# A two-layer decoder trunk on one core: x summed in PSUM over the expert sets, 21 weight slots, another load order

## The chip, the cores and the metric

One Trainium2 core runs the whole program. The metric is device time in microseconds (us); the profile is one execution of it. PE is TensorE, DVE VectorE, ACT ScalarE, POOL GpSimd, and SP the engine that issues nearly all the DMAs.

## What is computed

Two layers (DEPTH) over 256 tokens of width 1024, float32. A layer is an attention part and a mixture-of-experts (MoE) part, cut here to the second:

```
x = x + concat[diff attention, stick breaking attention](rms_norm(x)) @ w_out
h2 = rms_norm(x, norm2_g)
# top-1 of 4 expert groups, then top-2 of its 8 experts; 32 experts in all
hg = h2 @ w_gate[e];  hu = h2 @ w_up[e]          # (256, 1024) @ (1024, 256)
x = x + sum_e (silu(hg) * hu * combine[:, e]) @ w_down[e]
```

The weights are read once: 96 MiB of expert matrices in each layer (32 experts, three matrices of 1 MiB), and 16 MiB of w_in and w_out.

## The kernel before

**Slots.** SBUF holds 19 slots of 1 MiB (`wbuf`, SLOT). A slot takes one expert's gate, up or down matrix, or half of one 2 MiB column block of w_in or w_out. An expert set is 4 experts (LANES); 8 sets (SETS) make a layer. A set needs 12 slots. Gate matrices have 8 slots, 4 for each parity of the set; up matrices have 7 (the fourth, slot 9, is shared by both parities); down matrices have 4, shared by both parities. `hT` (the transposed, normed x) and `xn` (the normed x) lie in buffers of their own beside the slots.

**One set.** Each expert of a set gets 32 token places (SLOTS). PE multiplies gathered tokens `hgT` by gate and up (L1366, 128 matmul records), gathers the tokens of the next set by selection matrices (`gather`, L1341), transposes the routing weights (L1350) and the activations (L1387), multiplies by down (L1398) and scatters the result back to token order (L1410, 4 matmuls of 128x512). DVE then adds each of the four scattered blocks to `x_sb` (`into_x`, L916), and PE's next transposes of weights wait for that (`x_moe`). If an expert of a set has more than 32 tokens, `further` runs another round with its own tiles (L1377 is its gate and up). Sets 0 and 1 come in fixed order; sets 2 to 7 are sorted by their fullest expert, fullest first, and in both layers set 2 alone has a second round.

**Routing.** After attention's output projection (L1310), PE computes the router logits (`router`, L1317) and DVE runs a chain of some 30 small instructions from L1057 to L1156. On its way it signals `sel_ready` (PE gathers set 0) and at its end `routed`: only then does PE read the number of tokens and enter the loop over sets, and SP learn which experts sets 2 to 7 are.

**SP's queue.** SP issues DMAs in program order, with waits. `load_first_sets` issues all 12 slots of set 0 and gate and the first three up of set 1 (19 slots) during attention. `load_further_sets` waits for `routed`, reads six numbers and then goes through the sets with waits on `gate_used`, `up_used` and `dn_used`, which ACT counts up when PE has finished with the gate, up and down matrices of a set.

**The first block.** w_in's first 2 MiB block comes in two halves; PE's first projection (L1207) waits for the first, transposes the second half of x, then waits for the rest. Between the first and second projection PE computes `rstd_rows` (L1218) from `rstd_diag` (L994), which DVE makes after it has waited for `gains_in`, six small loads.

## Time and profile before

| | us |
|---|---|
| median of 3 runs | 745.71 (744.35 to 745.98) |
| the profiled execution | 742.31 |
| its span, in which all positions below lie | 740.5 |
| PE busy | 652.9 (88%) |
| DVE busy | 305.3 (41%) |
| ACT busy | 119.0 (16%) |
| HBM read | 237.51 MB, 322 GB/s over the span |

A position such as 170.03 is in microseconds from the start of the span. Layer 0's attention runs to about 153, its routing to 165 and its sets to 374; layer 1's routing is at 515 to 528 and its sets end with the span. PE's busy share is high everywhere, since records of pipelined matmuls touch each other; what limits a stage has to be read from the waits and the DMA rows.

### The profile page before, as it was taken

What the parts mean: (1) busy time and instruction counts of PE and PEld (TensorE: products, weight loads), DVE (VectorE), ACT (ScalarE), POOL (GpSimd) and SP (SyncE); (2) the same over time, 40 slices, a digit from 0 to 9 for tenths busy, and PEclk for the clock granted to TensorE, in tenths of its full rate; (3) what the DMA queues carried; (4) which work ended last, traced back from release to release, by engine and by line L of the source; (5) the groups of instructions that cost most, each with busy time, mean ns of one, the idle gap of its engine ahead of it and who ended that gap; (6) DMA issues with size and microseconds to landing.
All of it is one profiled execution on the core that took longest, in us unless ns stands there. A gap on an engine that the chain in (4) does not pass through costs nothing.

```text
span 740.5 us, 12416 instructions
## 1 busy us (share of the span) xinstructions
PE 652.9 (88%) x4796; PEld 374.1 (51%) x4797; DVE 305.3 (41%) x625; ACT 119.0 (16%) x284; POOL 9.0 (1%) x19
## 2 busy tenths in 40 slices
PE   7999999988798897784999999999898979785966
PEld 4478555475554353432345864546644535443522
DVE  0445663164353443431424377422633434432413
ACT  3103442220000000000031035324000000000000
POOL 0002000000000000000020000000000000000000
PEclk9999999999999998987999999999999999987989
DMA  8798426537999999999999630395299999999995
GB/s 307 264 335 304 169 113 277 234 115 295 415 422 416 393 423 421 421 422 423 388 357 395 271 144 28 129 382 222 67 377 420 422 421 423 422 423 420 423 406 208
DMA packets 52967, 239.09 MB, mean 323 GB/s; under 512 B 7824, under 2 KB 8112, under 8 KB 29376
## 3 DMA queue, kind: packets, MB, share of 16 engines
q1 hardware_dynamic: 52432, 238.14, 80.6%
q0 software_dynamic: 496, 0.44, 0.5%
q8 instruction: 23, 0.38, 0.2%
q14 instruction: 16, 0.13, 0.0%
HBM read 237.51 MB, written 1.05 MB: 322 GB/s over the span
## 4 chain that ended last, share of the span: by engine, by line
PE 67%; DMA 19%; DVE 5%; issue 4%; SPq 2%; DVEq 2%; ACT 1%; ACTq 0%
DMA wbuf<-in_w_down 18%; PE bank L1207 13%; PE bank L1398 11%; PE bank L1366 8%; PE bank L1197 8%; PE bank L1310 7%; PE bank L1410 5%; PE bank L1341 5%; PE bank L1377 2%; DMA wbuf<-in_w_in 1%; SPq L371 1%; PE bank L1266 1%; PE bank L1317 1%; PE bank L1240 1%; PE bank L1286 1%
## 5 line engine op out<-in xcount | busy, mean ns | idle before, releaser
L1398 PE MATMUL bank<-wbuf,qkT 128*32 128x512 f32 x512 | 73.2, 708 | 53.3 <-DMA wbuf<-in_w_down 46.5
L1207 PE MATMUL bank<-wbuf,hTbuf 128*128 128x512 f32 x256 | 114.7, 603 | 3.9 <-DMA wbuf<-in_w_in 3.5
L1366 PE MATMUL bank<-wbuf,qkT 128*32 128x256 f32 x2048 | 113.8, 380 | 2.2 <-DVE qkT L880 2.2
L1366 PEld LDWEIGHTS bank<-wbuf,qkT 128*32 128x32 f32 x2048 | 65.2, 110 | 54.2 <-issue 10.6
L1207 PEld LDWEIGHTS bank<-wbuf,hTbuf 128*128 128x128 f32 x256 | 48.3, 192 | 63.0 <-issue 58.9
L1341 PE MATMUL bank<-qkT,xn 128*128 128x128 f32 x512 | 62.9, 282 | 11.3 <-issue 10.4
L916 DVE TENSOR_TENSOR x_sb<-x_sb,bank 128x512 f32<-128x512 f32 x72 | 49.5, 688 | 51.0 <-PE bank L1410 51.0
L1341 PEld LDWEIGHTS bank<-qkT,xn 128*128 128x128 f32 x512 | 59.9, 196 | 18.4 <-issue 18.4
L1398 PEld LDWEIGHTS bank<-wbuf,qkT 128*32 128x32 f32 x512 | 19.2, 126 | 97.0 <-issue 86.9
L1197 PE MATMUL bank<-hTbuf,wbuf 128*128 128x256 f32 x256 | 56.5, 380 | 0.0
L1310 PE MATMUL bank<-wbuf,hTbuf 128*128 128x512 f32 x128 | 56.1, 594 | 0.0
L1197 PEld LDWEIGHTS bank<-hTbuf,wbuf 128*128 128x128 f32 x256 | 48.2, 190 | 7.0 <-issue 0.7
L908 DVE COPY qkT<-bank 128x512 f32<-128x512 f32 x16 | 11.1, 692 | 77.8 <-PE bank L1398 77.8
L1310 PEld LDWEIGHTS bank<-wbuf,hTbuf 128*128 128x128 f32 x128 | 23.8, 190 | 28.1 <-issue 28.1
L890 DVE RECIPROCAL qkT<-qkT 128x256 f32<-128x256 f32 x18 | 31.6, 1753 | 1.4
L1410 PE MATMUL bank<-qkT 128*128 128x512 f32 x64 | 29.9, 611 | 2.3 <-DVEq L969 2.3
L606 ACT COPY qkT<-bank 128x512 f32<-128x512 f32 x16 | 9.4, 586 | 134.5 <-PE bank L1398 134.5
L1410 PE MATMUL bank<-qkT,hTbuf 128*128 128x512 f32 x64 | 30.3, 616 | 0.0
L904 DVE COPY qkT<-bank 128x256 f32<-128x256 f32 x16 | 6.8, 425 | 53.9 <-PE bank L1387 53.9
L602 ACT ACTIVATE qkT<-bank 128x256 f32<-128x256 f32 x18 | 6.9, 385 | 126.9 <-PE bank L1366 113.1
L1410 PEld LDWEIGHTS bank<-qkT 128*128 128x128 f32 x64 | 11.0, 189 | 21.5 <-issue 17.7
L1410 PEld LDWEIGHTS bank<-qkT,hTbuf 128*128 128x128 f32 x64 | 10.8, 189 | 19.9 <-issue 14.7
(218 smaller groups left out, 564.5 us busy)
## 6 DMA issues: line engine op xcount, KB each, us to landing
wbuf<-in_w_gate SPq DMA_DIRECT2D x64, 1024.0 KB, 14.9
wbuf<-in_w_up SPq DMA_DIRECT2D x64, 1024.0 KB, 17.7
wbuf<-in_w_down SPq DMA_DIRECT2D x56, 1024.0 KB, 14.6
wbuf<-in_w_in SPq DMA_DIRECT2D x24, 1024.0 KB, 14.7
wbuf<-in_w_out SPq DMA_DIRECT2D x8, 1024.0 KB, 6.3
wbuf<-in_w_down SPq DMA_DIRECT2D x16, 512.0 KB, 7.8
x_sb<-in_x SPq DMA_DIRECT2D x2, 512.0 KB, 6.3
out<-x_sb SPq DMA_DIRECT2D x2, 512.0 KB, 2.6
```

What stands on the lines that cost most here:

```text
L606: nc.scalar.copy(dst[:, HALF:], ps[bank][:, :]).then_inc(s["y_a"], 1)
L890: V.reciprocal(rg, rg)
L908: V.tensor_copy(dst[:, 0:HALF], ps[bank][:, :]).then_inc(s["y_d"], 1)
L916: last.append(V.tensor_tensor(x_sb[:, t, c], x_sb[:, t, c], ps[SC_BANK[t][h]][:, :], ALU.add))
L1197: last = MM(ps[PROJ_BANK[i][t]][:, a * SEQ:(a + 1) * SEQ], block_rows(i, k)[:, cols], hT[:, k, :], start=(k == 0), stop=(k == KC - 1))
L1207: last = MM(ps[PROJ_BANK[i][t]][:, :], hT[:, k, t * P:(t + 1) * P], block_rows(i, k), start=(k == 0), stop=(k == KC - 1))
L1310: last = MM(ps[OP_BANK[t][h]][:, :], hT[:, k, t * P:(t + 1) * P], block_rows(i, k), start=(k == 0), stop=(k == KC - 1))
L1341: last = MM(ps[k // 4][:, (k % 4) * P:(k % 4 + 1) * P], xn[:, t, k * P:(k + 1) * P], sel[:, t, :], start=(t == 0), stop=(t == TT - 1))
L1366: last = MM(ps[bank][j * SLOTS:(j + 1) * SLOTS, 0:FF], hgT[:, k, j * SLOTS:(j + 1) * SLOTS], halves[:, at[j], k, :], start=(k == 0), stop= ...
L1377: last = MM(ps[MORE_GU][j * SLOTS:(j + 1) * SLOTS, :].rearrange("p (a f) -> p a f", a=2), hgT_more[:, k, j * SLOTS:(j + 1) * SLOTS], halve ...
L1398: last = MM(ps[banks[h]][j * SLOTS:(j + 1) * SLOTS, :], src[:, c, j * SLOTS:(j + 1) * SLOTS], at[j][:, c * D + h * HALF:c * D + (h + 1) * ...
L1410: MM(ps[SC_BANK[t][h]][:, :], weights[:, t, :], src[:, h * HALF:(h + 1) * HALF], start=True, stop=True).then_inc(s[f"sc{t}{h}_ps"], 1)
```

## The change

- **21 slots.** `xn` and `hT` lose their own buffers and become slots 19 and 20. Slot 19 is then set 1's fourth up matrix, slot 20 the first down matrix of the odd sets. So gate and up are fully double, and the first down matrix too. In attention the same memory serves as `xa` and `hT`, and after it as weights: SP loads up (1,3) after `oT_ps` and down (1,0) after `lg_ps`.
- **x in PSUM.** `keep_x` writes x into four PSUM banks by an identity matmul (4 of 128x512 per layer); every set's scatter accumulates there, and DVE and ACT copy the four banks to `x_sb` once per layer. `into_x` and the `x_moe` waits go. The normed x for the gathers is written over `x_sb` by ACT (`normed_to_x`), after `keep_x`, by way of `xn_first`.
- **Load order.** For set g+1: gate, then all four up, and only then the other three down of set g and the first down of g+1. For the last set down comes before up, and its halves are three instead of four. SP reads one expert number per set, where it read six ahead.
- **Routing.** PE enters the loop after `first_counts`, some ten DVE instructions ahead of `routed`. DVE scales the first half of the gathered set 0 before it sorts the sets, ACT the second half (`first_gathering`). In the loop PE reads the next count after up, not after its activation transposes, and transposes this set's weights there.
- **Router by column halves.** The last token tile of x is transposed and routed in two column halves, with the parameters loaded to match (11 small loads instead of 8).
- **First block in pieces.** The first 1 MiB half of block 0 becomes four DMAs with a semaphore each.
- **PE's loop placed.** In layer 1's second projection 128 semaphore increments stand between the matmuls, which shift all later code of PE.
- A second round shares `hgT`, `y` and the banks of the first, so its scatter ends before the first round's down starts.

```diff
-SLOTS_W = 19
+SLOTS_W = 21
-UP_SLOT = [[4, 5, SLOT_STAGE, 9], [6, 7, 8, 9]]
-DOWN_SLOT = [10, 11, SLOT_VALUES, 16]
+UP_SLOT = [[4, 5, SLOT_STAGE, 9], [6, 7, 8, SLOT_XN]]
+DOWN_SLOT = [[10, 11, SLOT_VALUES, 16], [SLOT_HT, 11, SLOT_VALUES, 16]]
...
             with act.If(most <= SLOTS):
+                act.wait_ge(first["gu_ps"], act.snap(n * LANES))
                 act.sem_inc(gate_used, 1)
             gate(first, n, FIRST_GATE)
...
+            def load_start():
+                for k in range(KC // 2):
+                    sp_.dma_start(dst[:, k, :], src[:, k, :]).then_inc(start_in[k], 16)
...
+            def keep_x(t):
+                for h in range(2):
+                    last = MM(ps[X_BANK[t][h]][:, :], ident, x_sb[:, t, h * HALF:(h + 1) * HALF], start=True, stop=False)
+                last.then_inc(x_kept, 1)
...
+            def scatter(s, n, weights, last):
+                for h in range(2):
+                    pe.wait_ge(s["y_a" if h else "y_d"], n)
+                    for t in range(TT):
+                        mm = MM(ps[X_BANK[t][h]][:, :], weights[:, t, :], y[:, h * HALF:(h + 1) * HALF], start=False, stop=last)
+                        if last:
+                            mm.then_inc(x_ps[t][h], 1)
...
+            def place_loop(n):
+                for _ in range(n):
+                    pe.sem_inc(placed, 1)
...
+                    if l > 0 and i == 1:
+                        place_loop(8)
...
+                # after up, inside the loop
+                pe.wait_ge(routed, l + 1)
+                pe.reg_mov(count, pe.value_load(cnt[0:1, bass.ds(SETS - 1 - g, 1)], min_val=0, max_val=SEQ))
+                transpose_weights(first, n, SELW_BANK)
```

**SP, from the last loads of layer 0's attention to the first ones behind `routed`.** Before:

```order
L368 DMA wbuf<-in_w_up 128x2048
L368 DMA wbuf<-in_w_up 128x2048 [waits oproj_ps]
L368 DMA wbuf<-in_w_up 128x2048
L420 TENSOR_LOAD sorted_i [waits routed]
L420 ISA x2
```

And now:

```order
L364 DMA wbuf<-in_w_up 128x2048 [waits oT_ps]
L360 DMA wbuf<-in_w_gate 128x2048 [waits oproj_ps]
L364 DMA wbuf<-in_w_up 128x2048
L364 DMA wbuf<-in_w_up 128x2048 [waits oproj_ps]
L364 DMA wbuf<-in_w_up 128x2048
L368 DMA wbuf<-in_w_down 128x2048 [waits lg_ps]
L423 TENSOR_LOAD sorted_i [waits routed]
L423 ISA x2
```

One up matrix and one down matrix (1 MiB each) have moved ahead of the wait for `routed`.

**SP, the first turn over the sets, behind the last gate matrix of set 2.** Before:

```order
L364 DMA wbuf<-in_w_gate 128x2048
L368 DMA wbuf<-in_w_up 128x2048 [waits up_used]
L371 DMA wbuf<-in_w_down 128x2048 [waits dn_used]
L371 DMA wbuf<-in_w_down 128x2048 x3
L368 DMA wbuf<-in_w_up 128x2048 x3
L368 DMA wbuf<-in_w_up 128x2048 [waits up_used]
L364 ISA [waits gate_used]
```

And now:

```order
L360 DMA wbuf<-in_w_gate 128x2048
L364 DMA wbuf<-in_w_up 128x2048 [waits up_used]
L364 DMA wbuf<-in_w_up 128x2048 x3
L368 DMA wbuf<-in_w_down 128x2048 [waits dn_used]
L368 DMA wbuf<-in_w_down 128x2048 x3
L423 TENSOR_LOAD sorted_i
L423 ISA x2
L360 ISA [waits gate_used]
```

Eight loads stand between `gate_used` and the wait for `dn_used`, where five stood.

**PE, from the gather of set 0 to its first expert matmul.** The tile qkT holds the selection and the gathered tokens. Before:

```order
L1341 MATMUL bank0<-qkT,xn 128x128 [waits sel_ready,xn_ready]
L1341 MATMUL bank0<-qkT,xn 128x128 x7
L1341 MATMUL bank1<-qkT,xn 128x128 x8
L1350 MATMUL bank6<-cst,qkT 128x128 [waits selw_ready]
L1350 MATMUL bank6<-cst,qkT 128x128
L1549 TENSOR_LOAD sorted_i [waits routed]
L1549 ISA x2
L1550 UNCONDITIONAL_BRANCH
L1550 ISA
L1357 ISA [waits gate_in0]
L1366 MATMUL bank2<-wbuf,qkT 32x256 [waits hg0]
```

And now:

```order
L1379 MATMUL bank0<-qkT,x_sb 128x128 [waits sel_ready,xn_ready]
L1379 MATMUL bank0<-qkT,x_sb 128x128 x7
L1379 MATMUL bank1<-qkT,x_sb 128x128 x8
L1593 TENSOR_LOAD sorted_i [waits first_counts]
L1593 ISA x2
L1594 UNCONDITIONAL_BRANCH
L1594 ISA
L1395 ISA [waits gate_in0]
L1404 MATMUL bank2<-wbuf,qkT 32x256 [waits hg0]
```

The weight transposes have left this place, and the register load waits for an earlier semaphore.

## Rows read from the trace of the kernel before

**Rows 1.** The page: what DMA moved in 40 slices, and the chain by line.

```profile
GB/s 307 264 335 304 169 113 277 234 115 295 415 422 416 393 423 421 421 422 423 388 357 395 271 144 28 129 382 222 67 377 420 422 421 423 422 423 420 423 406 208
...
DMA wbuf<-in_w_down 18%; PE bank L1207 13%; PE bank L1398 11%; PE bank L1366 8%; PE bank L1197 8%; PE bank L1310 7%; PE bank L1410 5%; PE bank L1341 5%; PE bank L1377 2%; DMA wbuf<-in_w_in 1%; SPq L371 1%; PE bank L1266 1%; PE bank L1317 1%; PE bank L1240 1%; PE bank L1286 1%
```

**Rows 2.** Stretches: length, PE, PEld, DVE, ACT, POOL busy, PEclk, DMA share, GB/s.

```profile
160.00:165.00 5.00, 4.03 (x34) 3.82 (x34) 3.97 (x21) 0.37 (x1) 0.00 (x0) 1.00 0.00 0
...
170.00:175.00 5.00, 5.00 (x70) 3.85 (x63) 2.79 (x3) 0.00 (x0) 0.00 (x0) 1.00 0.77 285
...
180.00:185.00 5.00, 5.00 (x33) 1.62 (x26) 1.85 (x4) 0.59 (x1) 0.00 (x0) 1.00 0.99 383
185.00:190.00 5.00, 5.00 (x72) 2.60 (x74) 2.58 (x6) 0.00 (x0) 0.00 (x0) 1.00 0.99 398
...
245.00:250.00 5.00, 3.67 (x8) 1.44 (x8) 2.76 (x4) 0.35 (x1) 0.00 (x0) 1.00 0.86 311
...
545.00:550.00 5.00, 5.00 (x25) 1.58 (x19) 2.44 (x4) 0.59 (x1) 0.00 (x0) 1.00 0.93 346
```

**Rows 3.** Timeline of SP's DMA issues: start, length, instruction, count.

```profile
170.03 2.12 SPq L364 DMA_DIRECT2D wbuf<-in_w_gate  x4
...
182.96 2.68 SPq L371 DMA_DIRECT2D wbuf<-in_w_down  x4
...
231.28 2.08 SPq L364 DMA_DIRECT2D wbuf<-in_w_gate  x4
244.71 2.07 SPq L371 DMA_DIRECT2D wbuf<-in_w_down  x4
...
532.27 3.37 SPq L364 DMA_DIRECT2D wbuf<-in_w_gate  x4
```

**Rows 4.** The chain of waits, layer 0 from routing to set 2.

```profile
164.07 0.03 DVEq L1157
...
165.42 7.11 PE bank L1366 x128
...
193.53 5.18 issue
...
212.16 7.04 PE bank L1366 x128
219.20 0.02 issue
```

**Rows 5.** Timelines, layer 0's routing and second round, then layer 1: idle time before in brackets.

```profile
150.90 0.59 ACT L532 COPY hTbuf<-bank 128x512 f32<-128x512 f32 x1 [0.49 <-PE bank L1170]
...
156.99 0.43 PE L1328 MATMUL bank<-oh,cst 128*128 128x64 f32 x2 [0.77 <-DVEq L1098]
...
160.20 3.81 PE L1341 MATMUL bank<-qkT,xn 128*128 128x128 f32 x32 [0.43 <-DVEq L1122]
...
223.28 7.07 PE L1377 MATMUL bank<-wbuf,hTbuf 128*32 128x512 f32 x64
...
528.09 7.11 PE L1366 MATMUL bank<-wbuf,qkT 128*32 128x256 f32 x128 [0.99 <-DVE qkT L880]
...
582.53 7.07 PE L1377 MATMUL bank<-wbuf,hTbuf 128*32 128x512 f32 x64
```

**Rows 6.** The in-loop register load of PE by its line: min/median/max ns, first and last start.

```profile
L1459 PEldq TENSOR_LOAD <-sorted_i x16: 298/312/318, 177.6 to 727.6; - x16
```

**Rows 7.** The start: timelines of PE and DVE, with the idle time before.

```profile
10.32 5.40 PE L1207 MATMUL bank<-wbuf,hTbuf 128*128 128x512 f32 x8 [3.55 <-DMA wbuf<-in_w_in]
...
16.43 10.46 PE L1207 MATMUL bank<-wbuf,hTbuf 128*128 128x512 f32 x24
...
26.23 0.48 DVE L994 TENSOR_SCALAR wbuf<-cst,rstd 128x128 f32<-128x128 f32 x2 [9.35 <-DMA lamv<-in_lambda_k]
```

**Rows 8.** The chain of waits at the end of the span.

```profile
731.08 1.92 PE bank L1398 x16
733.01 3.73 PE bank L1410 x8
```

More of the change, by code:

```diff
@@ L594, in sb_scales, with weights_copy, first_gathering @@
                 nc.scalar.activation(osq[:, 2 * t + 1, :], osq[:, 2 * t + 1, :], ACT.Exp, scale=-0.5).then_inc(o_rT, 1)
-            def weights_copy(s, n, dst, half):
+            def weights_copy(s, n, dst, bank):
                 act.wait_ge(s["selwT_ps"], n)
-                nc.scalar.copy(dst.rearrange("p t s -> p (t s)"), ps[SELW_BANK][:, half]).then_inc(s["selwT_out"], 1)
+                nc.scalar.copy(dst.rearrange("p t s -> p (t s)"), ps[bank][:, 0:TT * P]).then_inc(s["selwT_out"], 1)
+            def first_gathering(l):
+                act.wait_ge(first["gathered1"], l * SETS + 1)
+                for k in range(4, 8):
+                    last = nc.scalar.activation(hgT[:, k, :], ps[1][:, (k - 4) * P:(k - 3) * P], ACT.Copy,
+                                                scale=g2T[:, k:k + 1])
+                last.then_inc(first["hg1"], 1)
             def gate(s, n, bank):
@@ L1403, in scatter, with down @@
-            def scatter(s, n, weights, src):
-                pe.wait_ge(s["selwT_out"], n)
-                pe.wait_ge(s["y_d"], n)
-                for t in range(TT):
-                    for h in range(2):
-                        if t == 0 and h == 1:
-                            pe.wait_ge(s["y_a"], n)
-                        MM(ps[SC_BANK[t][h]][:, :], weights[:, t, :], src[:, h * HALF:(h + 1) * HALF],
-                           start=True, stop=True).then_inc(s[f"sc{t}{h}_ps"], 1)
+            def down(s, n, parity, src, h, second_half=None):
+                if h == 1 and second_half is not None:
+                    pe.wait_ge(last_dn_in, second_half)
+                at = [slot(DOWN_SLOT[parity][j]) for j in range(LANES)]
+                for c in range(FC):
+                    for j in range(LANES):
+                        last = MM(ps[DN_BANK[h]][j * SLOTS:(j + 1) * SLOTS, :], src[:, c, j * SLOTS:(j + 1) * SLOTS],
+                                  at[j][:, c * D + h * HALF:c * D + (h + 1) * HALF], start=(c == 0), stop=(c == FC - 1))
+                        if c == FC - 1:
+                            last.then_inc(s[f"dn{h}_ps"], 1)
@@ L1542, in _ @@
                 router(l, 1, 1)
-                keep_clock(12)
+                for t in range(TT):
+                    keep_x(t)
                 ranks(l)
```

364 lines of the change are left out of this document (186 added, 178 removed).

## The prediction

> **What bounds the kernel now.** I read the slices of the page first. In the expert sets (slices 11 to 20 and 31 to 39) DMA moves about 421 GB/s, in attention far less [rows 1]. The chain names a down matrix as its largest part: late sets wait for weights. The chain of a layer's first sets is PE's, but DMA is at full rate there too. So I take DMA as the bound of the sets from the moment it restarts after routing, and ask three things: when it restarts, how many slots are then missing, and where it pauses.
>
> A slot of 1 MiB at 421 GB/s takes 2.49 us, a set of 12 slots 29.9. PE needs for a set 7.04 for gate and up, 3.81 for the gather, twice 1.92 for down, 3.73 for the scatter [rows 4, 5, 8] and about 1.2 of small steps: 19.6. It is ahead except at the start of a layer.
>
> - *Restart.* From 160 to 165 DMA moves nothing [rows 2]: all 19 slots are full. SP issues set 2's gate matrices at 170.03 in layer 0 and at 532.27 in layer 1 [rows 3]. That follows the gate matmuls of set 0 (half of the 7.11 us from 165.42 [rows 4], so done at 168.98) and ACT's exponential, 1.05 us later. Until data flows some 2 us pass (170 to 175 lacks 136 of 421 GB/s, 1.6 us).
> - *Missing.* 96 - 19 = 77 slots, 191.7 us.
> - *Pauses.* In layer 0 180 to 190 lacks 38 and 23 GB/s over 5 us each, 0.7 us: down could be issued only at 182.96. 245 to 250 lacks 110, 1.3 us: down at 244.71, after set 2's two rounds. In layer 1 545 to 550 lacks 75, 0.9 us [rows 2, 3].
> - Set 3's gate matrices go out at 231.28, behind set 2's second round (223.28 + 7.07 = 230.35) [rows 3, 5]. DMA has 24 slots to move until there: 170.03 + 2 + 59.8 + 0.7 = 232.5. PE and DMA meet there almost exactly.
>
> **The change part by part.**
>
> *Two more slots: -5.0 us in each layer.* Up (1,3) is issued behind `oT_ps`, down (1,0) behind `lg_ps`; they need 5 us of DMA, which stands empty before the restart. After it 75 slots are missing instead of 77. DMA sets the end, so 2 x 2.49 = 5.0 is all gain.
>
> *Earlier restart: layer 0 -2.0, layer 1 -1.4.* Before, PE entered the loop 1.35 us after `routed` (164.07 to 165.42) [rows 4]. Now its register load waits for `first_counts`, which DVE gives at about 160.8, and PE's sequencer can run it while the gather (160.20 to 164.01 [rows 5]) is in the array: the first in-loop load begins at 177.6 [rows 6], while the gather and transposes before it end at 178.6. The first half of `hgT` is ready near 163.1. ACT's second half starts at 164.0, in four pieces, about 1.2 by the 0.59 us of a copy of 512 columns [rows 5] and twice that at most for short ones; it is needed at 164.05 + 1.8. So gate starts at 164.05, 1.4 earlier; in layer 1 1.1 earlier, since 528.09 lies nearer to its gather's end. ACT signals `gate_used` ahead of its exponential: another 0.3 to 0.6. `routed` itself comes 0.75 later, by the half gather put before the sort, at about 164.9; that is still ahead of gate's end, 167.6.
> Against it stand `keep_x` and ACT's two copies: 4 matmuls of 0.86 from about 153.5, done at 156.95, where the next matmul waits until 156.99 [rows 5] behind filler matmuls; ACT's copies of 1024 columns, 1.2 each, end near 158.3, before the gather at 160.20. I take nothing; without this cover it would be some 0.4.
>
> *Load order: layer 0 -1.3 and -0.7, layer 1 -0.9.* Eight slots (19.9 us) lie between `gate_used` and the wait for down, where five lay (12.4). The pauses go.
>
> *Who sets set 3's gate in layer 0?* DMA would need it issued by 168.0 + 2 + 59.8 - 2 = 227.8. PE is there at 230.35 - 1.4, plus 0.25 for the weight transposes now ahead of the second round: 229.2, issued at 230.1, 1.2 earlier than before. So PE decides, and of 2.0 + 0.7 only 1.2 is left: layer 0 gains 1.2 + 5.0 + 1.3 = 7.5. Layer 1 reaches its second round sooner (582.53 - 528.09 = 54.4 us after its first gate, against 57.9 [rows 4, 5]) and restarts 0.2 later behind that gate: DMA decides, 1.4 + 5.0 + 0.9 = 7.3.
>
> *Second round in turn, no `x_moe`, 64 adds replaced by 8 copies: 0.* PE's steps stay in number, and DVE had slack in every set. If the register load shows behind up, it costs 0.8 in each of three sets that lead to 230: bounds 0 to 2.4. I take 0, since the up matmuls queue ahead of it as the gather does in rows 6.
>
> *Router by halves: 0.* PE runs the same instructions in another order, and is busy throughout. Bounds -0.2 to 0.
>
> *First block in pieces: 0, with a bound above.* PE could start at 8 instead of 10.32 and finish the first projection near 24.6 (the second half of the block and x land near 14.3, then 24 records take 10.4 [rows 7]). But L1218 needs DVE's L994, which waits until 26.23 for a small load [rows 7]. The time saved is waited off again, and PE idles 2.3 us. It idled 3.55 before 10.32, and the eight records after took 5.40 us for 3.44. If the clock falls to 1.2 GHz behind this idle time too, 1.7 is lost. Range -0.1 to +1.7; I take 0.
> The Trainium skill (TensorE: Matmul & The Clock Gate, The HAM clock gate) says that half rate is PE's default and activity releases it; by that rule 1.7 goes into the sum, which gives 733. The row at 10.32 agrees for a longer idle time; no row shows 2.3 us.
>
> *128 semaphore increments: 0.* Eight stand between two matmuls of 0.87 us. An entry of this sort takes about 0.03 (as DVE's at 164.07 [rows 4]) and as much to the next, so eight are about 0.5, under the matmul. If none is covered: 128 x 0.07 = 9 us, the upper bound. I take 0, for PE's sequencer runs ahead of the array [rows 6].
>
> *Placement and fetches: 0, range -2 to +5.* Layer 0's set 1 loses 5.18 us at 193.53 to "issue"; at 219.20 the same place costs 0.02 [rows 4]. The new loop has one more branch. If the stall goes, DMA and not PE decides at 231 and layer 0 gains 2 more. If another comes in the first three sets, up to 5 are lost.
> The Trainium skill (Runtime: NRT & Kernel Launch, Instruction fetch mechanics) says that a taken branch out of the fetched window forces a fetch before the engine goes on. By that rule every set would stall at the skipped second round; the row at 219.20 shows a turn without. What it would do here is the rival below.
>
> *Tail: +0.3.* Down 1.92 and scatter 3.73 [rows 8] stay. The last add becomes a copy of the same size, but x's first tile is complete after the third scatter instead of the second, so its output load leaves 0.9 later.
>
> **Sum**: -7.5 - 7.3 + 0.3 = -14.5. Against its own execution: 742.31 - 14.5 = 727.8 (span 726.0). The median of the runs lies 3.4 above that execution: 745.71 - 14.5 = 731.2.
>
> **Rivals.**
> - *PE reaches the first releases late (0.22).* The register loads show (2.4) and a fetch stall of up to 5 comes in one layer. For it: 5.18 in rows 4. Against: layer 1 was 3.4 quicker. 731.2 + 4 to 8, say 737.
> - *The clock falls at the start (0.10).* 733, within the forecast's own range.
> - *Fetches in every set (0.07), slower.* The place is the skip over the second round and the new branch before the last scatter. PE's 19.6 us must exceed DMA's 29.9, so it decides from 10.3 us of stall per set, two of 5.18. At 12 us the twelve late sets lose 1.7 each, 20 in all: 751. For it: the stall exists. Against: 0.02 at 219.20.
> - *The change does nothing (0.03).* The increments would cost 9 and a stall 5: 745.
> - *The forecast (0.58)*, its own range 728 to 735.
>
> **How the numbers follow.** 0.2% is 1.5 us, about what a measurement of this kernel can tell. Forecast and the first two rivals are faster, 0.90, less a little for their tails: 0.88; same 0.04, slower 0.08. The range goes from the forecast with the stall gone (728) to a little over the first rival (739).
>
> **What would show it.** Right: 21 slots loaded before SP's wait for `routed`; SP's first loop issue at 168.0 in layer 0, and no stretch under 400 GB/s from there to the last set except near 230; L1218 again near 26.9 with PE idle before it. Wrong: a first gate matmul later than 165, "issue" of several us in the first sets, or layer 1's second projection longer than 13.9 us (16 matmuls of 0.87).

## Result and profile after

| | before | after |
|---|---|---|
| median | 745.03 us of 4 runs | 725.58 us of 4 runs (723.18 to 728.31) |
| ratio | | 0.9754, 95% interval 0.9725 to 0.9783 |
| the profiled execution (span) | 742.31 (740.5) | 726.92 (725.1) |

The change makes the kernel some 18 us faster by the ratio (0.0246 x 745.0 = 18.3); the two medians differ by 19.5. I had forecast 14.5 and a median of 731.2, in a range from 728 to 739. The direction is right, the gain was put too small: 725.58 lies below the range. The two profiled executions differ by 15.4.

The page of the changed kernel: slices of DMA, and the queue through which instructions are fetched (packets, MB, share).

```profile
GB/s 318 260 292 355 183 116 225 296 233 277 420 421 400 414 426 421 420 423 423 395 353 394 260 136 54 116 397 230 162 420 419 421 373 423 422 423 421 422 418 208
...
q8 instruction: 23, 0.38, 0.2%
```

As before [rows 1], DMA is full in the sets. SP's issues in the changed kernel:

```profile
167.62 2.42 SPq L360 DMA_DIRECT2D wbuf<-in_w_gate  x4
170.82 1.78 SPq L364 DMA_DIRECT2D wbuf<-in_w_up  x4
180.29 2.15 SPq L368 DMA_DIRECT2D wbuf<-in_w_down  x4
...
228.61 1.93 SPq L360 DMA_DIRECT2D wbuf<-in_w_gate  x4
230.64 2.23 SPq L364 DMA_DIRECT2D wbuf<-in_w_up  x4
248.50 1.76 SPq L368 DMA_DIRECT2D wbuf<-in_w_down  x4
...
522.61 2.04 SPq L360 DMA_DIRECT2D wbuf<-in_w_gate  x4
...
700.47 4.68 SPq L373 DMA_DIRECT2D wbuf<-in_w_down  x6
```

The first issue is at 167.62 (forecast 168.0, before 170.03 [rows 3]), set 3's gate at 228.61 (230.1, 231.28). Stretches of the changed kernel, columns as in [rows 2]:

```profile
160.00:165.00 5.00, 5.00 (x60) 4.34 (x63) 3.46 (x17) 1.14 (x4) 0.00 (x0) 1.00 0.00 0
...
180.00:185.00 5.00, 5.00 (x36) 2.24 (x36) 0.71 (x3) 0.59 (x1) 0.00 (x0) 1.00 1.01 421
...
245.00:250.00 5.00, 5.00 (x36) 1.65 (x29) 1.40 (x4) 0.59 (x1) 0.00 (x0) 1.00 1.01 421
250.00:255.00 5.00, 5.00 (x65) 2.50 (x67) 0.00 (x0) 0.00 (x0) 0.00 (x0) 1.00 0.98 387
545.00:550.00 5.00, 4.69 (x72) 3.02 (x65) 3.08 (x4) 0.76 (x2) 0.00 (x0) 1.00 1.01 418
```

The pauses at 180 (383 before), 245 (311) and 545 (346) are gone. I had expected no stretch under 400 GB/s except near 230. There are others: 387 from 250 to 255, and in layer 1 362 and 297 from 580 to 590, because set 3's gate goes out only at 584.95. There PE decided, where I had put DMA; a1 below has 426 and 419 at this place. PE's timeline, its start, layer 0's first sets, layer 1's second projection (382.36) and the end:

```profile
26.64 0.67 PE L1246 MATMUL bank<-wbuf,cst 128*128 128x256 f32 x2 [2.60 <-DVEq L1002]
...
163.53 7.11 PE L1404 MATMUL bank<-wbuf,qkT 128*32 128x256 f32 x128
...
176.50 3.64 PE L1434 MATMUL bank<-wbuf,qkT 128*32 128x512 f32 x32 [1.61 <-issue]
...
197.19 3.36 PE L1379 MATMUL bank<-qkT,x_sb 128*128 128x128 f32 x14 [3.81 <-issue]
...
235.78 5.34 PE L1434 MATMUL bank<-wbuf,further_tiles 128*32 128x512 f32 x32 [2.57 <-issue]
...
382.36 13.90 PE L1235 MATMUL bank<-wbuf 128*128 128x512 f32 x32
...
715.29 1.92 PE L1434 MATMUL bank<-wbuf,qkT 128*32 128x512 f32 x16 [0.64 <-DMA wbuf<-in_w_down]
717.15 3.70 PE L1443 MATMUL bank<-qkT 128*128 128x512 f32 x8
```

PE has its first gate matmul at 163.53 (forecast 164.05, before 165.42 [rows 4]); the last down ends its wait for DMA at 715.29, where it was 731.08 [rows 8]. Layer 1's second projection, with the 128 increments in it, takes 13.90 us in this timeline, what layer 0's takes from 27.15 on without any, so the 128 increments cost no time of their own.

### The profile page after: what moved, and what is told of

It reads as the page before. It is cut to its first block, busy times and chain, and to the rows that moved or that the text cites. A ratio compares the mean times of both kernels' runs of the same rounds, so it can differ in the third digit from the quotient of the medians.

```text
span 725.1 us, 12394 instructions
## 1 busy us (share of the span) xinstructions
PE 651.3 (90%) x4764; PEld 371.4 (51%) x4765; DVE 257.7 (36%) x557; ACT 126.3 (17%) x298; POOL 11.0 (2%) x22
## 4 chain that ended last, share of the span: by engine, by line
PE 71%; DMA 17%; issue 4%; SPq 3%; DVE 3%; ACT 1%; DVEq 1%; ACTq 0%
DMA wbuf<-in_w_down 15%; PE bank L1235 12%; PE bank L1434 10%; PE bank L1404 10%; PE bank L1221 8%; PE bank L1379 8%; PE bank L1338 8%; PE bank L1443 6%; PE bank L1415 2%; DMA lamv<-in_lambda_k 2%; PE bank L1346 1%; PE bank L1294 1%; SPq L373 1%; PE bank L1268 1%; PE bank L1314 1%
## 5 line engine op out<-in xcount | busy, mean ns | idle before, releaser
L1235 PE MATMUL bank<-wbuf 128*128 128x512 f32 x256 | 113.1, 596 | 3.4 <-ACT wbuf L547 1.9
L1379 PE MATMUL bank<-qkT,x_sb 128*128 128x128 f32 x576 | 71.4, 284 | 11.1 <-issue 10.2
L1235 PEld LDWEIGHTS bank<-wbuf 128*128 128x128 f32 x256 | 47.7, 190 | 61.4 <-issue 57.1
L1379 PEld LDWEIGHTS bank<-qkT,x_sb 128*128 128x128 f32 x576 | 68.5, 198 | 14.3 <-issue 14.2
L1443 PE MATMUL bank<-qkT 128*128 128x512 f32 x128 | 59.2, 605 | 0.0
L1221 PE MATMUL bank<-wbuf 128*128 128x256 f32 x256 | 56.5, 380 | 0.0
L1338 PE MATMUL bank<-wbuf 128*128 128x512 f32 x128 | 56.1, 594 | 0.0
L1221 PEld LDWEIGHTS bank<-wbuf 128*128 128x128 f32 x256 | 48.2, 190 | 7.0 <-issue 0.7
L623 ACT COPY qkT<-bank 128x512 f32<-128x512 f32 x18 | 10.5, 586 | 200.1 <-PE bank L1434 200.1
L907 DVE TENSOR_SCALAR qkT<-qkT 128x256 f32<-128x256 f32 x18 | 5.3, 294 | 109.4 <-ACT qkT L619 109.4
L1443 PEld LDWEIGHTS bank<-qkT 128*128 128x128 f32 x128 | 23.0, 189 | 36.6 <-issue 29.1
L1338 PEld LDWEIGHTS bank<-wbuf 128*128 128x128 f32 x128 | 23.9, 190 | 28.1 <-issue 28.1
L896 DVE TENSOR_TENSOR qkT<-bank,g2T 128x512 f32<-128x512 f32 x34 | 22.0, 682 | 6.9 <-PE bank L1379 6.7
L577 ACT ACTIVATE wbuf<-wbuf,dmax 128x128 f32<-128x128 f32 (+1 forms) x32 | 14.1, 442 | 33.0 <-DVE dmax L801 32.8
## 6 DMA issues: line engine op xcount, KB each, us to landing
wbuf<-in_w_in SPq DMA_DIRECT2D x23, 1024.0 KB, 14.5
```

The lines of the kernel that those rows point to most:

```text
L577: last = nc.scalar.activation(s, s, ACT.Exp, bias=dmax[:, u, c:c + 1], accum_out=dsum[:, u, c:c + 1])
L896: V.tensor_tensor(hgT[:, 4 * h:4 * h + 4, :], ps[h][:, :].rearrange("p (k s) -> p k s", k=4), g2T[:, 4 * h:4 * h + 4].unsqueeze(2).broadca ...
L1221: last = MM(ps[PROJ_BANK[i][t]][:, a * SEQ:(a + 1) * SEQ], block_rows(i, k)[:, cols], hT[:, k, :], start=(k == 0), stop=(k == KC - 1))
L1235: last = MM(ps[PROJ_BANK[i][t]][:, :], hT[:, k, t * P:(t + 1) * P], block_rows(i, k), start=(k == 0), stop=(k == KC - 1))
L1338: last = MM(ps[OP_BANK[t][h]][:, :], hT[:, k, t * P:(t + 1) * P], block_rows(i, k), start=(k == 0), stop=(k == KC - 1))
L1379: last = MM(ps[k // 4][:, (k % 4) * P:(k % 4 + 1) * P], xn[:, t, k, :], sel[:, t, :], start=(t == 0), stop=(t == TT - 1))
```

## Experiments

All medians in one table. "Before" beside them had medians of 743.5 to 744.9 in the same sessions; nearly all its executions lie between 740 and 750. A loss in us below is the difference of two medians; where the two runs come from different sessions it can be off by about 1 us, and by the ratios some losses come out smaller (e6 1.4 instead of 1.8, e7's gain 2.1 instead of 2.6, e4 5.3 instead of 7.1). The last column counts the packets of the instruction queue in the page, 16 KB each.

| run | median us | ratio to before, 95% | packets |
|---|---|---|---|
| a1, changed kernel again | 724.30 | 0.9741 (0.9703, 0.9778) | 23 |
| b1, before again | 744.21 | 1.0004 (0.9975, 1.0034) | 23 |
| e1, no increments | 771.35 | 1.0359 (1.0313, 1.0405) | 50 |
| p4, 64 increments | 724.25 | 0.9737 (0.9695, 0.9779) | 23 |
| p16, 256 increments | 793.32 | 1.0653 (1.0607, 1.0699) | 51 |
| e3, before with 128 | 778.37 | 1.0444 (1.0394, 1.0494) | 51 |
| q1, before with 256 | 745.27 | 1.0024 (0.9993, 1.0055) | 24 |
| q4, layer 0 moved by 64 | 772.46 | 1.0376 (1.0336, 1.0416) | 50 |
| q6, layer 0 moved by 16 | 723.30 | 0.9725 (0.9686, 0.9765) | 23 |
| e2, two slots late | 734.85 | 0.9880 (0.9842, 0.9917) | 23 |
| e4, entry behind routed | 731.37 | 0.9812 (0.9773, 0.9851) | 23 |
| e5, downs before ups | 742.57 | 0.9982 (0.9953, 1.0011) | 23 |
| q2, one up ahead | 735.32 | 0.9883 (0.9842, 0.9923) | 23 |
| q3, slots, entry, order undone | 743.69 | 0.9991 (0.9964, 1.0018) | 23 |
| q5, last set as the others | 746.41 | 1.0033 (1.0008, 1.0057) | 23 |
| e8, four undone | 790.13 | 1.0617 (1.0571, 1.0662) | 50 |
| e6, first load whole | 726.11 | 0.9760 (0.9718, 0.9802) | 23 |
| e7, small loads waited for later | 721.68 | 0.9713 (0.9674, 0.9752) | 23 |

### Two further profiles of the same kernels (a1, b1)

> The changed kernel once more, unchanged, to see how far its executions lie apart and where. The first pair of profiled executions differs by 15.4 us, the two sets of runs by about 18. Theory A (the terms of the sum are right for one execution; single executions differ by some 3 us either way, because stalls named issue and stretches at half clock fall in different places): the second profile shows stalls of 1 to 5 us in other sets than the first, the last down matrix lands between 712 and 719 us, and the ratio to the kernel before is 0.975 to 0.980. Theory B (a term is too small by 3 to 4 us in every execution): both profiles show the same landings within 0.5 us.

> The kernel before once more, unchanged, for a second profile of it. The changed kernel's executions differ in when the small load of lambda lands (VectorE ends its wait for it between 24.10 and 26.24 us in five profiles), and the first projection's second half starts right behind it. Theory A: in the kernel before TensorE comes to this place at 26.9 anyway, so a landing at 24 to 26 moves nothing, and its median of about 745 lies above its first profiled 742.31 for another reason: a half-clock stretch in the first microseconds or a stall in a set that the first profile lacks, worth 1.7 to 3 us. Rival: the two profiles agree within 0.5 us at every place, and the first was simply the low end of noise in DMA.

Places of the profiles, in us. Profiles whose program is the same up to the end of a stretch are taken together (layer 1's loop of q1 lies as in the kernel before, modulo 256 entries):

| stretch | before | changed | difference | forecast |
|---|---|---|---|---|
| start to layer 0's first gate matmul | 165.42, 165.18, 164.89, 165.36 | 161.65 to 164.49, nine profiles, mean 163.1 | -2.1 | -1.4 |
| to layer 0's last down matmul | 204.3, 205.9, 205.1, 209.4 | 197.9, 197.9, 198.2, 198.0, 198.4 | -8.1 | -6.1 |
| layer 1's first projection to first gate | 151.80 | 150.37 | -1.4 | -1.1 |
| to layer 1's last down matmul | 204.3, 206.0, 202.7 | 198.1, 196.2, 196.3 | -7.5 | -6.2 |
| tail and between the layers | | | +0.5 | +0.3 |

The sum is 18.6, which agrees with the ratio. So theory A holds for half: executions differ by 2 to 5 us, and the pair of single profiles understates the gain by 3. b1, the second profile of the kernel before, is 3.0 us longer than the first, 1.6 of it in layer 0's sets and 1.7 in layer 1's: the first profile was a short one. But the terms are too small too, by 0.7, 2.0, 0.3 and 1.3.

What DMA lacks against 421 GB/s, summed over windows of 2.5 us from set 2's gate issue to the last landing of the layer and given as time in us, says where (means of the same profiles as above; the stretches left out lack nothing):

| after set 2's gate issue | layer 0: before, changed | layer 1: before, changed |
|---|---|---|
| 0 to 10 us | 1.6, 1.7 | 2.6, 1.6 |
| 10 to 25 us | 1.3, 0.0 | 0.9, 0.0 |
| 50 to 90 us | 1.8, 1.5 | 0.0, 0.7 |
| from 170 us on | 2.0, 0.8 | 3.5, 2.1 |
| in all | 6.6, 3.9 | 6.7, 4.3 |

The time that is left, at 2.49 us a slot, is 77.8 slots before and 75.8 now in layer 0, 77.1 and 75.1 in layer 1: the two slots are there to a tenth. The pauses give 2.7 and 2.4 us. My sum left 0.5 of them in layer 0 (0.7 + 1.3, less 1.5 because PE decides at set 3's gate) and 0.9 in layer 1. What I had not counted is the last stretch of each layer (1.1 and 1.4) and layer 1's slower restart before the change (1.0, where I took 2 us for both kernels). What I had counted in layer 0 from 10 to 25 us, 0.7, lies between 0.5 and 2.1 in the four profiles.

### The first block (e6, e7)

> The changed kernel with the first half block of weights in one load again. Theory A (the pieces gain between 0.2 and 2 us, by when the small load of lambda lands, since TensorE is done with its first 32 matmuls at 23.3 to 24.0 instead of 26.9): 1 to 1.5 us slower than the changed kernel in the median, and the wait at the second half's first matmul gone. Rival (the forecast: waited off, nothing): within 0.3 us.

e6 puts the first half block back into one load, with a wait on its first matmul alone. e7:

```diff
-                dve.wait_ge(gains_in[l], N_GAINS)
                 dve.wait_ge(norm_r, 4 * l + TT)
...
                 gap().then_inc(diag_ready, 1)
+                dve.wait_ge(gains_in[l], N_GAINS)
```

> The changed kernel with VectorE's wait for the small loads moved behind diag_ready, so that TensorE's second half of the first projection needs no lambda. Theory A: it starts at about 23.5 to 24.7 instead of 24.9 to 27.2, 1 to 2 us faster in the median than the changed kernel, if nothing else of VectorE's is late (the norms of q and k behind it need lambda only at the end). Rival (a half-clock stretch at the start comes or goes with TensorE's idle time and outweighs this): no difference, or 1 us slower.

PE's timeline, first of a1, then of e6, then of e7:

```profile
12.76 10.57 PE L1235 MATMUL bank<-wbuf 128*128 128x512 f32 x24 [0.46 <-DMA wbuf<-in_w_in]
24.93 0.67 PE L1246 MATMUL bank<-wbuf,cst 128*128 128x256 f32 x2 [1.60 <-DVEq L1002]
```

```profile
9.41 6.73 PE L1234 MATMUL bank<-wbuf 128*128 128x512 f32 x8 [3.35 <-DMA wbuf<-in_w_in]
...
27.17 0.59 PE L1245 MATMUL bank<-wbuf,cst 128*128 128x256 f32 x2
```

```profile
12.66 10.57 PE L1234 MATMUL bank<-wbuf 128*128 128x512 f32 x24 [1.06 <-DMA wbuf<-in_w_in]
23.07 0.60 PE L1245 MATMUL bank<-wbuf,cst 128*128 128x256 f32 x2
```

With the pieces PE is done with its first 32 records at 23 to 24 and waits for DVE, whose small load lands anywhere between 24.1 and 26.2: 26.64 in the first profile, 24.93 here, 25.8 as the mean of twelve. Without them PE itself is there at 26.4 to 26.9 (four profiles of the kernel before) or 27.17 (e6). The first profile had the load late, and so agreed with "waited off again" by chance. e6 is 1.8 us slower in the median, as theory A had it, and e7 2.6 faster. Both intervals overlap a1's, so for e6 the profiles are the better witness. For e7 they settle it: e7, q4 and q6, which share this edit, reach the first gate at 159.9, 160.2 and 160.0, and the nine profiles in the table above at 161.65 at the earliest.

The rival of the clock is real too. In three of these twelve profiles (e4, p16, q2) the granted clock fell to half, from 2.4 to 1.2 GHz, behind PE's wait (in e4 its mean from 25 to 30 us is 0.66 of full speed, in the first profile 1.00); PE's timeline of e4, where 32 records take 15.59 instead of 13.90:

```profile
25.53 0.67 PE L1246 MATMUL bank<-wbuf,cst 128*128 128x256 f32 x2 [2.00 <-DVEq L1002]
26.04 15.59 PE L1235 MATMUL bank<-wbuf 128*128 128x512 f32 x32
...
166.21 8.78 PE L1404 MATMUL bank<-wbuf,qkT 128*32 128x256 f32 x128 [2.03 <-issue]
```

That is the 1.7 us of the forecast's bound. It came behind 2.00 us of idle time here (1.98 in p16, 2.33 in q2) and not behind 2.60 in the first profile or 2.85 in q3, so the length of the wait alone does not decide it. In e7 and its two relatives, with no idle time at this place, it did not come.

### Slots, entry and order

e2 moves two lines, e4 changes one:

```diff
-                sp_.wait_ge(oT_ps, (l + 1) * TT)
-                load_up(l, 1, 3)
...
-                sp_.wait_ge(lg_ps, (l + 1) * TT)
-                load_down(l, 1, 0)
...
                         sp_.wait_ge(gate_used, l * SETS + g)
+                        if g == 1:
+                            load_up(l, 1, 3)
+                            load_down(l, 1, 0)
```

```diff
-                pe.wait_ge(first_counts, l + 1)
+                pe.wait_ge(routed, l + 1)
```

> The changed kernel with the two extra slots (the last up matrix and the first down matrix of set 1) loaded only behind set 1's gate_used, so 19 slots lie there at the restart as before. Theory A: 2 x 2.49 us of DMA come back in each layer, so 10 us slower than the changed kernel (8 to 10, since in layer 0 PE decides part of the way). Rival (the slots are worth less, because DMA pauses in the sets anyway and takes them up there): 2 to 5 us slower.

> The changed kernel with PE's loop entered behind routed, as before the change, instead of behind first_counts. Theory A: set 0's first gate matmul is 1.3 to 1.9 us later in each layer, DMA restarts as much later, and the kernel is 2.5 to 3.8 us slower. Rival (the first counts bring nothing, since the gather and hgT decide): within 1 us. Theory B (the stalls of the first turns hang on where the register load stands): slower by 5 us or more, with a stall of over 3 us in set 0 or 1 that the changed kernel lacks.

e2 is 10.5 us slower, for a forecast of 5.0 a layer. e4 is 7.1 slower in the median, 3.3 more than theory A's upper end; its six executions lie from 728.2 to 731.9. The row at 166.21 shows one reason in the profiled one: PE idles 2.03 us and then has set 0's gate at half clock, 8.78 us for 7.11, on top of the 1.7 lost at 26. Two more profiles with this entry have the same wait, and the clock falls behind it in one (e8) and not in the other (q3). In e4's layer 1, where the clock stays, gate comes 2.2 later than in a1 (152.54 after the first projection against 150.37) and the sets take no more time than in a1.

e5 and q2 take the loop's order back, e5 to no up ahead of the downs, q2 to one as before. This is q2's edit; e5's puts all four ups behind:

```diff
                     if g + 1 < SETS - 1:
                         sp_.wait_ge(up_used, l * SETS + g)
-                        for j in range(LANES):
-                            load_up(l, g + 1, j)
+                        load_up(l, g + 1, 0)
...
                         load_down(l, g + 1, 0)
+                        if g + 1 < SETS - 1:
+                            for j in range(1, LANES):
+                                load_up(l, g + 1, j)
```

> The changed kernel with the loop's down matrices issued ahead of the up matrices in all sets, the order of before. The prediction gave the new order 1.3 + 0.7 us in layer 0 and 0.9 in layer 1, from DMA's three pauses. Theory A (as measured so far the sets gained 7.5 and 8.1 us, of which the two slots are 5.2 and 4.0): the order is worth 2 to 3 us in each layer, so this kernel is 4 to 6 us slower than the changed one. Rival (the forecast's term): 1.5 to 3 us slower in all. Either way DMA should show a pause where down is issued late.

> The changed kernel with one up matrix ahead of the wait for the downs and three behind, so five loads between gate_used and that wait, as before the change, instead of eight (four cost 18 us). By the forecast's term: 1.2 + 0.7 us in layer 0 and 0.9 in layer 1, 3 us slower in all. By the other theory (DMA now restarts earlier and has two slots fewer to fill, so TensorE comes to the second round later against it, and the wait for dn_used costs more than it did before): each load ahead covers 2.49 us, the pause with four was 2.3 + 5.8 in layer 0, so with five about 3.3 remains there and more in layer 1, 7 to 9 us slower.

e5 is 18 us slower and q2 11.0, where the forecast's term would be 3. Where four loads lie ahead of the downs (e5), one less than before the change, DMA loses more still. Stretches of q2, then of a1:

```profile
240.00:245.00 5.00, 5.00 (x34) 1.70 (x36) 0.66 (x1) 0.00 (x0) 0.00 (x0) 1.00 0.67 280
245.00:250.00 5.00, 5.00 (x32) 1.80 (x24) 0.74 (x4) 0.58 (x1) 0.00 (x0) 1.00 0.57 193
600.00:605.00 5.00, 5.00 (x36) 1.32 (x34) 0.69 (x1) 0.00 (x0) 0.00 (x0) 1.00 0.31 128
605.00:610.00 5.00, 5.00 (x36) 2.24 (x36) 0.70 (x3) 0.58 (x1) 0.00 (x0) 1.00 0.73 257
```

```profile
240.00:245.00 5.00, 5.00 (x28) 1.68 (x30) 0.00 (x0) 0.10 (x1) 0.00 (x0) 1.00 1.02 426
245.00:250.00 5.00, 5.00 (x24) 1.70 (x16) 1.40 (x4) 0.59 (x1) 0.00 (x0) 1.00 0.96 393
```

DMA runs dry behind set 2's second round. In the kernel before, 13.4 us lie between set 3's gate issue and the downs (231.28 to 244.71 [rows 3]), five loads' worth and 1 us more. In the new loop it is 18.2 in q2 (SP's row of down is at 246.09, its gate at 227.90) and 19.9 in the changed kernel. The second round's scatter (3.70) now lies inside this stretch, and its down matmuls wait 2.57 us in every profile of the new loop. In the kernel before the same place waited 1.83:

```profile
237.46 3.64 PE L1398 MATMUL bank<-wbuf,hTbuf 128*32 128x512 f32 x32 [1.83 <-DVE hTbuf L904]
```

So the scatter is most of the 4.8 us. The step from 18.2 to 19.9 is the clock again: the 32 down records behind the wait take 5.34 us in the row at 235.78, and 3.64 in q2. Eight loads, 19.9 us, cover either. So the second round in turn, which I costed at nothing, makes this stretch some 5 us longer, and what hides it is the new order. No run puts the second round's old order back, so its price in time is worked out from these rows and not measured. In the new loop the order is worth 11; that it would be worth 3 in the old one is my forecast, which no run tests.

> The changed kernel with the two slots late, the loop entered behind routed and one up matrix ahead of the downs, with the increments in place: what is left of the change is the start, the half gathers and the second round in turn. By the sum of the forecast's terms this is 14.8 less 0.3, so 14 us slower than the changed kernel. If the three move the same restart and overlap: 8 to 11. If the order costs more in the new loop (q2): 17 to 20, and so the kernel before itself was helped by a faster first pair of sets.

q3 is 19.4 slower than a1 and level with the kernel before, though the single losses add to 28.6: with the two slots late, DMA has 5 us more to move when it comes to the second round, so the pause there should shrink, and it does: 2.1 us in layer 0 (245 to 255) and 2.6 in layer 1 (610 to 615), against q2's 4.4 and 5.4. What is left in q3 is the start, x in PSUM, the router by halves, the second round in turn, the half gather ahead of the sort and the last pair's order. Together they give nothing in the median; single ones can still cancel. x in PSUM was not undone alone in any run.

q5 takes back the last pair's order alone:

```diff
-                    if g + 1 < SETS - 1:
+                    if g + 1 < SETS:
                         sp_.wait_ge(up_used, l * SETS + g)
                         for j in range(LANES):
                             load_up(l, g + 1, j)
...
-                        if g + 1 == SETS - 1:
-                            sp_.wait_ge(up_used, l * SETS + g)
-                            for j in range(LANES):
-                                load_up(l, g + 1, j)
```

> The changed kernel with the last pair of sets loaded in the order of the others (ups ahead of downs). If the order at the end is a term of its own: set 6's downs land four loads (10 us) later, so TensorE frees the slots of the last downs up to 10 us later than at 696.1, where DMA had 6 to 7 us of work left; DMA then pauses 2 to 4 us in layer 1 right before the last landing, and the kernel is 2 to 4 us slower. Rival (the end is DMA's whatever the order, as the forecast had it): within 0.5 us.

It is 22.1 us slower. Against a1's profile that is 9.5 in layer 0's sets and 10.7 in layer 1's, with 1.7 from the clock in between. SP's issues and the stretches of layer 1 in q5:

```profile
690.83 1.76 SPq L368 DMA_DIRECT2D wbuf<-in_w_down  x4
719.39 4.61 SPq L373 DMA_DIRECT2D wbuf<-in_w_down  x6
```

```profile
710.00:715.00 5.00, 0.83 (x5) 0.24 (x9) 0.00 (x0) 0.00 (x0) 0.00 (x0) 0.52 0.86 357
715.00:720.00 5.00, 5.00 (x34) 1.57 (x27) 0.69 (x1) 0.56 (x1) 0.00 (x0) 0.79 0.01 5
720.00:725.00 5.00, 5.00 (x51) 2.32 (x53) 0.00 (x0) 0.02 (x1) 0.00 (x0) 1.00 0.80 258
```

The last downs wait until PE is through set 6's, and those now land four loads later. DMA stands still meanwhile. Measured from the first gate matmul, the last downs go out at 191.6 us in q5, 179.4 in a1, and at 187.8 and 189.7 in the two profiles of the kernel before (715.85 and 719.11), which shows a smaller lack of the same kind. The stretches of b1:

```profile
715.00:720.00 5.00, 5.00 (x27) 1.87 (x20) 0.69 (x1) 0.58 (x1) 0.00 (x0) 0.68 0.82 342
720.00:725.00 5.00, 5.00 (x55) 2.35 (x57) 2.75 (x4) 0.00 (x0) 0.00 (x0) 1.00 0.85 260
725.00:730.00 5.00, 4.68 (x88) 2.58 (x80) 2.64 (x4) 0.38 (x1) 0.00 (x0) 1.00 1.04 373
```

Against 421 that is (79 + 161) x 5 / 421 = 2.9 us in the first two stretches. The first profile of the kernel before lacks 1.0 there (386 and 368 GB/s). The forecast had no term for the last pair; the table above puts the difference to the changed kernel at 1.1 and 1.4 us a layer.

### The place of the loop (e1, p4, p16, e3, q1, q4, q6, e8)

```diff
-                    if l > 0 and i == 1:
-                        place_loop(8)
```

> The changed kernel without the 128 semaphore increments that stand before layer 1's matmuls of the second projection. Theory A: their own cost is nothing and nothing else moves, so the time stays within 1.5 us of the changed kernel's. Theory B (the place of PE's loop in memory decides whether its turns stall, which is where the 3 to 4 us beyond the forecast come from): 3 us slower or more, with more or longer idle times named issue in the sets than the 1.1, 3.8, 2.3 us in layer 0 and 1.9, 3.4, 2.3 us in layer 1 of the first profile.

e1 is 47 us slower, nearly all of it in layer 1's sets (242.9 us against 196.2 to 198.1). PE's timeline there, one set and the gather of the next:

```profile
653.35 1.07 PE L1402 MATMUL bank<-wbuf,qkT 128*32 128x256 f32 x7 [4.10 <-issue]
658.68 9.17 PE L1402 MATMUL bank<-wbuf,qkT 128*32 128x256 f32 x121 [4.26 <-issue]
667.79 0.44 PE L1386 MATMUL bank<-cst,qkT 128*128 128x128 f32 x2
673.44 5.55 PE L1377 MATMUL bank<-qkT,x_sb 128*128 128x128 f32 x32 [5.21 <-issue]
...
698.14 2.07 PE L1377 MATMUL bank<-qkT,x_sb 128*128 128x128 f32 x8 [3.73 <-issue]
```

A pair of sets stalls 4.10 + 4.26 + 5.21 + 3.73 = 17 us, and the clock halves behind the stalls (9.17 us for 121 of the 128 records that take 7.11 at full clock). On the page the instruction queue has 50 packets where the changed kernel has 23, and the other 27 all lie from 570 on. The DMA view of the changed kernel from 160 to 210, that is its first pair of sets, has this row, and from 210 to 360 there is none for this queue:

```profile
q8 instruction: 6, 0.10, 0.8%
```

and that of e1 from 570 to 765:

```profile
q8 instruction: 27, 0.44, 0.9%
```

The profile does not say which engine a packet is for; that these are PE's is inferred, since it is PE that stalls, and only where they keep coming. By that reading PE in a good place fetches its loop during the first turn (a turn is a pair of sets), and then runs it without a fetch; in a bad one it fetches in every turn to the end. q4 shows the same in layer 0: 27 packets more than in e7, all from 210 on.

> The changed kernel with 64 increments instead of 128. Theory A (only the loop's place in memory matters, and stalls come in every set when the loop lies wrongly, gradually less as it is moved): between 724 and 771 us, with stalls named issue in every set of layer 1 if over 735. Rival (the place matters by a threshold): either 724 or 771 within 3 us. Theory C (the increments work by their time beside the matmuls, not by their place): half of the gain, 748.

> The changed kernel with 256 increments instead of 128. Theory A (place): another place, which may be good or bad; if bad, stalls of 3 to 5 us come in every set of layer 1 at other matmuls than without increments, 10 to 50 us slower. Theory C (the increments' own effect): as the changed kernel or faster, 724 or less. Their own cost shows in layer 1's second projection, 13.9 us with 128 of them: with 256, 16 before each matmul of 0.87 us, it grows if 16 take longer than that.

> The kernel before with the 128 semaphore increments alone, put ahead of the matmuls of layer 1's second projection. Without them the changed kernel is 47 us slower, all of it in layer 1's sets, where stalls named issue of 3.4 to 5.4 us come in every set. If it is the place of layer 1's loop in memory that decides, the kernel before has a good place now, and moving it by these 128 entries can spoil it: 10 to 45 us slower, with such stalls in layer 1's sets and none new in layer 0's. Rival (the increments help by themselves, or only in the changed loop): within 1.5 us of the kernel before.

> The kernel before with 256 increments, eight before each matmul of two of layer 1's projections, so that none costs time of its own. If the place repeats with 256 entries (in the changed kernel 0 and 256 show the same stalls, 4 us behind the seventh of a set's gate matmuls): as the kernel before within 1.5 us, 744, though 128 made it 34 us slower. If the place only gets worse with distance, or the increments themselves do harm: 30 us slower or more.

64 is as good as 128 (724.25), 256 as bad as none, with its stalls at the same place: 4.04 us ahead of a set's gate (at 675) and 4.62 behind its seventh record (at 681), where e1 has 4.10 and 4.26. (256 also cost 19 us of their own, since sixteen ahead of each matmul set most of them 2.44 us apart instead of 0.87: layer 1's first gate comes 169.7 us after the first projection, against 150.4. Two of p16's rows:

```profile
396.16 2.05 PE L1235 MATMUL bank<-wbuf 128*128 128x512 f32 x2 [0.40 <-issue]
398.60 2.04 PE L1235 MATMUL bank<-wbuf 128*128 128x512 f32 x2 [0.40 <-issue]
```

> The kernel with the later wait for the small loads (721.7 us) and four increments before each matmul of the second projection in both layers: layer 0's loop is moved by 64 entries and layer 1's by 128 in all, as in the changed kernel. If the stalls of layer 0's sets (1.5, 3.8 and 2.6 us at about 175, 193 and 234) hang on its place, they change; DMA lacks some 1.5 us around 230 and 250 there, so at best 720, and at worst stalls in every set and 20 us more. If layer 0's place is no worse or better: 721.7 within 1 us.

> The kernel with the later wait for the small loads (721.7 us), one increment before each matmul of layer 0's second projection (16 entries) and four in layer 1's (80 in all there). If the loop's place matters by where a set's branches fall in steps of some tens of entries: layer 0's stalls stay those of place 0 (about 1.5, 3.2 to 4.2, 2.6 us in its first sets) or turn into those of place 64 (5 us in every set, 45 us slower). If 16 is between, the kernel lies between 721 and 770.

q4 loses 51 us against e7, all in layer 0 (248.7 us for its sets instead of 197); q6 is within its scatter of e7. Layer 0's loop lies well at 0 and at 16 entries and badly at 64.

> The changed kernel with four parts undone at once: no increments, the two slots late, the loop entered behind routed, downs before ups. It has the changed kernel's loop without its placement, so as far as layer 1's stalls set the end it should be near the kernel without the increments (771 us) and not at the sum of the single losses (724 + 47 + 10.5 + 7 + 3): with DMA no longer the bound in layer 1, the slots are worth nothing there. In layer 0, where no stall comes in every set, the losses of slots, entry and order should add: 5.2 + 2 + 2 us, as one theory; the rival is that they overlap (all three move the same restart of DMA) and layer 0 loses 6 us or less. In all 778 to 786 us.

e8 lies above the range I gave: layer 1's sets take 249.3, 6 more than in e1, so there the other losses do not vanish beside the stalls. Layer 0 lost 3.3 up to its first gate against a1 (2.1 against the mean of the nine) and 11.0 in its sets, 13 to 14 in all where I had added up 9: its order is e5's, with only four loads ahead of the downs, and that costs more than the 2 us I put there (e5 loses 18 us over both layers).

The Trainium skill (Runtime: NRT & Kernel Launch, Instruction fetch mechanics) says that instructions come in blocks of 16 KiB, 256 each, and that a taken branch out of the fetched window forces a fetch before the engine goes on. The packets of 16 KB and the period of 256 agree with it. It also says that prefetch is purely sequential and that nothing gains from locality. The trace does not agree: in a good place the loop takes its branch back and has no packet for 150 us.

## Why the prediction was right in direction and too small

The sum of the terms was 14.5, the measured one is 18.6. The steps that failed are the size of the pauses, which were read from one execution and left out the last pair of sets and layer 1's restart (together 3.3 too small), and the first block, put at nothing, which is most of the 0.7 that the start is short.

- **Two more slots, 5.0 a layer: right.** Undone, 10.5 in all (e2), and DMA moves 2.0 slots less behind the restart in each layer.
- **Earlier restart: right in place, a little small.** First gate 1.4 us earlier in layer 1 (forecast 1.1), first issue within 0.4 of the forecast in the first profile. ACT's earlier signal brought 0.5 in layer 0 and 0.1 in layer 1 (forecast 0.3 to 0.6). Undoing the entry alone cost 7.1 in the median, partly through the clock, of which the forecast said nothing at this place.
- **Pauses and load order, 1.3 + 0.7 + 0.9: the pauses it named are gone, but the term is mis-sized.** Less DMA time is lost by 2.7 and 2.4 us a layer, where the sum left 0.5 and 0.9. It has no term for the last pair of sets (1.1 and 1.4), and it took 2 us for the restart of both kernels where layer 1 of the kernel before needs 1.0 more. It also read the pauses from the execution of 742.31, shorter than all the runs beside it (743.06 to 745.98), and applied them to a median of 745.71. The order's own price was wrong in another way: it was sized by the pauses of the old loop, while the new loop stretches the time between gate and down issues from 13.4 to 18 or 20 us. Without the new order the new loop loses 11 us (q2), and without the last pair's order alone 22 (q5). With the order in place neither loss appears, so this error did not move the total.
- **PE up to set 3's gate in layer 0, and placement, 0 with -2 to +5.** I had PE issue set 3's gate 66.05 us after the first gate matmul; it was 65.3 in the mean of five profiles, and 66.8 in four of the kernel before. Most of that is the stall in set 1, 5.18 in [rows 4]: 5.1 in the mean of four before, 3.8 of five now. Why it shrank is open. Layer 1's second round went the other way in the first profile (2.0 us lacking from 50 to 90), which I had given to DMA.
- **Second round in turn, 0: wrong as a price, right in effect.** It makes the stretch between the issues some 5 us longer; the order covers it.
- **First block in pieces, 0: the step that failed by relying on one landing.** DVE's small load at 26.23 [rows 7] was taken as fixed. It lies between 24.1 and 26.2, and the pieces gain about 1 us by the profiles, less 1.7 in one of four executions for the clock, and 1.4 to 1.8 by e6. That the first profile of the changed kernel showed "waited off again" was luck.
- **128 increments, 0: right**; for sixteen a matmul it would have been wrong, and my bound of 0.07 us each too low (2.44 us for sixteen and a matmul).
- **Fetches: right for this place, but the stake was far larger.** The rival of fetches in every set had the mechanism, but put 20 us on both layers, and e1 loses 47 in one. It asked for 10.3 us of stall a set before PE decides; e1 shows 17 a pair and loses all the same. That the stalled sets also release their slots late, and that the clock halves behind the stalls, fits the rows but was not separated. The rival stays away only because the loops lie well.
- **The step to the median.** The sum was made against the profiled 742.31 and gave 727.8 for that pair; 726.92 was measured. But the first profile of before lay low in its spread and the first of after high, so the agreement to 0.9 us hid a sum that was 4 too small.
- **Not tested by itself:** x in PSUM and the router by halves, both put at 0. q3 bounds them only together with the rest.

## What to carry to other kernels

A term that removes a pause has to be sized in the new order, not in the old one: ask what the distance between the two issues will be, and whether the same edit makes it longer. Undo each part alone and then together; here 28.6 became 19.4. And for an engine that runs a long loop, read the packet count of the instruction queue on the page before comparing two versions: 23 or 50 decides over more time than the whole change, and any edit ahead of the loop can flip it. The best version is e7, 721.68: a wait moved behind the work that doesn't need it. And size a pause from several executions: the same pause of the kernel before cost 0.5 to 2.1 us.

## What the hardware showed

- The place of PE's loop, modulo 256 entries, is worth 34 us (kernel before), 47 (layer 1) and 51 (layer 0). Only a few places were tried: 0, 64, 128 and 256 entries in layer 1 of the changed kernel, 0, 16 and 64 in its layer 0, 0, 128 and 256 in the kernel before.
- Eight semaphore increments ahead of a matmul of 0.87 us are free, sixteen stretch it to 2.44.
- The program up to the first projection is the same in twelve profiles. Half clock followed PE's wait there in three of them, at waits of 1.98, 2.00 and 2.33 us, and did not at 2.49, 2.60, 2.83 and 2.85. It costs 1.7 us.
- The small loads at the start land over a range of 2.1 us from one execution to the next.
